# First stage of a hybrid decoder step: conditioning weights loaded in one piece, scale first, sums before squares

## Chip, cores, metric

One core of a Trainium2 chip runs the whole step as one program. The metric is device microseconds of one execution, from launch to end; lower is better. Engines: TensorE (PE, its weight loads PEld), VectorE (DVE), ScalarE (ACT), GpSimd (POOL) and SyncE (SP), which here only issues DMAs.

## What is computed

A two-layer decoder trunk (a gated linear attention layer, then a recurrent RG-LRU layer, each followed by a product-key expert mixer) for 256 prompt tokens and 8 x 4 sample tokens. Only the start matters here: a condition vector for each of nine sequences goes through Silu and the conditioning weights of a layer, which gives six vectors; the first two are the shift and the scale of the first norm, whose result enters the first projection.

```
cond = jax.nn.silu(c)
mod = (cond @ p['ada_w'][i] + p['ada_b'][i]).reshape(B, 6, D_MODEL)
sh1, sc1, g1, sh2, sc2, g2 = [mod[:, j, None, :] for j in range(6)]
hm = rms_norm(x, p['norm_mix_g'][i]) * (1 + sc1) + sh1
mixed, s_new = gla_mixer(hm, ...)          # begins with hm @ w_in
x = x + g1 * mixed
```

## The kernel before

Everything lies with the feature dimension on 128 partitions: x, hid and the like are [128, 8, 288] (8 pieces of the 1024 features, 256 prompt and 32 sample tokens). Products that matter are made in three matmuls of split operands: a high part (a rounded copy, made by ScalarE) and a low part (value minus high part, made by VectorE, in some stages by GpSimd), for weights (w_hi, w_lo, lines 660 and 1566) and for activations (hid_hi, hid_lo).

All weights stream in chunks of [128, 1024] floats (512 KB) through raw, a ring of four slots. SyncE issues them in the order of the list SEGMENTS, each as soon as the slot's last user is done (mix_freed, freed). The order of work on every engine is written out by hand, and semaphores join the engines; a wait holds up all that stands behind it on its engine.

The first stage: the segment ada_a holds 16 chunks, group 0 (shift) and group 1 (scale) of eight each. ada_chunk (line 1084) makes four small matmuls for each, with the condition as stationary operand, into a PSUM bank. ScalarE copies the sums to ada_row in two halves (ada_half, line 632), TensorE turns them (line 1091), VectorE adds the bias and writes mod (mods, line 1688). The other groups are mixed in between the 24 chunks of the first projection (MIX_ITEMS) and between those of later stages.

Ahead of it, ScalarE issues seven loads (lines 616 to 622) and waits for five of them together; it then makes Silu of the condition and eight squares of x. TensorE sums the squares (square_sum, line 1075), runs four filling matmuls into the PSUM banks (line 1298) and then the 16 chunks. VectorE makes the mean, the root with ScalarE's help, and once it has both groups, the coefficient (1 + scale) x gain (norm_coef). It then splits the first two main weights (next_low) and applies the norm (norm_apply): in the first norm, eight products x * coefficient * root (line 1606), then eight additions of the shift (line 1623), with ScalarE's high copies (line 715) and VectorE's low parts (line 1611) following piece by piece.

GpSimd waits for the use of all 16 chunks (raw_used), issues the eight loads of the sample states (line 557, 512 KB each), and makes the sample columns of the norm in three operations (norm_samples, lines 483 to 488); after ScalarE's copy of them (line 712) it makes their low part (line 490). TensorE's wait for that (smp_low) opens the loop over the 24 tiles of the first projection (three, lines 1062 to 1064), which also holds conditioning chunks and pieces of the attention (gla_piece; at tile 3 the low-rank projection, line 1372, reads hid itself).

The arena is one large buffer in which the stages lay out their tensors one over the other. Its first 16384 floats in each partition are not in use before the first projection writes its results there.

## Time and profile before

| | us |
|---|---|
| three runs, median | 2246.83 |
| three runs, lowest to highest | 2246.06 to 2248.22 |
| profiled execution, own time | 2247.59 |
| its span, first to last instruction | 2245.8 |

The profiled execution's own time is 1.8 us above its span, and 0.8 us above the median. Over the span TensorE is busy 2094.1 us, VectorE 1603.4, ScalarE 1334.3 and GpSimd 963.5. Times in the rows are microseconds from the start of the span. A timeline row gives the start, the length, the engine, the line of the kernel and the operation, and in square brackets how long the engine stood idle before it and which work ended that. Rows of one line close together are merged, and their count stands behind x. A plain 4-byte matmul leaves two records. The granted clock is a share of 2.4 GHz: 0.50 is 1.2 GHz.

### The profile page before, as it was taken

The numbers are of one execution on the slowest core, as the hardware profiler recorded it, in microseconds if no ns is written. First come the engines' busy times: TensorE is split into PE (matmuls) and PEld (weight loads), VectorE is DVE, ScalarE is ACT, GpSimd is POOL, SyncE is SP. The second block draws the span as 40 slices with busy tenths as digits, with TensorE's granted clock in tenths as the row PEclk, the third lists the DMA queues.
The fourth block names the chain that finished last, engine by engine and source line by source line (L and its number), as shares of the span: only waits on it lengthen the run. The fifth ranks groups of instructions, "written<-read, shape, count | busy, mean of one in ns | idle before, by whom it ended". The sixth has DMA issues, their size and how long they took to land.

```text
span 2245.8 us, 42297 instructions
## 1 busy us (share of the span) xinstructions
PE 2094.1 (93%) x14238; PEld 1844.4 (82%) x14238; DVE 1603.4 (71%) x2994; ACT 1334.3 (59%) x2370; POOL 963.5 (43%) x818
## 2 busy tenths in 40 slices
PE   4998899999999999999989579898999999999998
PEld 1777898989999987777769479898999998777776
DVE  1446565796888878777867453949799998877785
ACT  1444443456777767667744534455777776766774
POOL 1010027777888732223300000888777773222330
PEclk7999999999999999999999889999999999999999
DMA  7753536666555568888844344454533446888883
GB/s 268 267 190 126 177 114 225 235 225 222 190 182 196 198 228 297 296 305 293 294 154 141 107 134 131 133 177 153 198 127 130 131 131 203 302 299 302 294 293 126
DMA packets 125618, 459.89 MB, mean 205 GB/s; under 512 B 14144, under 2 KB 14672, under 8 KB 124480
## 3 DMA queue, kind: packets, MB, share of 16 engines
q1 hardware_dynamic: 103104, 377.14, 49.8%
q0 software_dynamic: 21504, 79.53, 9.6%
q10 hardware_dynamic: 896, 1.76, 0.2%
q8 instruction: 65, 1.06, 0.2%
q14 instruction: 49, 0.40, 0.1%
HBM read 449.93 MB, written 8.44 MB: 204 GB/s over the span
## 4 chain that ended last, share of the span: by engine, by line
PE 74%; DVE 8%; issue 6%; POOL 6%; ACT 3%; DMA 3%; POOLq 0%; ACTq 0%; DVEq 0%; SPq 0%
PE pm L1264 11%; PE pm L1266 11%; PE pm L1265 10%; PE pu L1194 7%; PE pu L1189 7%; PE pu L1190 6%; PE pu L1062 4%; POOL w_lo L506 3%; PE pu L1064 3%; PE pu L1063 3%; PE pm L1224 2%; PE pm L1225 2%; POOL w_lo L545 1%; PE pm L1084 1%; PE pu L1509 1%
## 5 line engine op out<-in xcount | busy, mean ns | idle before, releaser
L1566 DVE TENSOR_TENSOR w_lo<-raw,w_hi 128x1024 fp32r<-128x1024 f32 x492 | 627.3, 1275 | 418.2 <-ACT w_hi L660 367.9
L660 ACT ACTIVATE w_hi<-raw 128x1024 fp32r<-128x1024 f32 x604 | 637.5, 1056 | 445.0 <-PE pm L1266 225.2
L1189 PE MATMUL pu<-hid_hi,w_hi 128*128 128x256 f32 x2048 | 504.9, 287 | 8.4 <-ACT w_hi L660 8.4
L1190 PE MATMUL pu<-hid_lo,w_hi 128*128 128x256 f32 x2048 | 496.2, 281 | 0.0
L1189 PEld LDWEIGHTS pu<-hid_hi,w_hi 128*128 128x128 f32 x2048 | 388.8, 190 | 34.3 <-issue 31.0
L1264 PE MATMUL pm<-w_hi,hid_lo 128*128 128x512 f32 x1024 | 403.6, 394 | 2.2 <-DVE hid_lo L1807 2.2
L1266 PE MATMUL pm<-w_lo,hid_lo 128*128 128x512 f32 x1024 | 402.4, 393 | 0.0
L1265 PE MATMUL pm<-w_hi,hid_lo 128*128 128x512 f32 x1024 | 401.6, 392 | 0.0
L1190 PEld LDWEIGHTS pu<-hid_lo,w_hi 128*128 128x128 f32 x2048 | 388.6, 190 | 0.0
L506 POOL TENSOR_TENSOR w_lo<-raw,w_hi 128x1024 fp32r<-128x1024 f32 x112 | 299.8, 2687 | 201.0 <-ACT w_hi L660 200.2
L1194 PE MATMUL pu<-hid_hi,w_lo 128*128 128x256 f32 x2048 | 294.6, 286 | 16.3 <-POOL w_lo L506 15.7
L1194 PEld LDWEIGHTS pu<-hid_hi,w_lo 128*128 128x128 f32 x2048 | 260.9, 190 | 21.4 <-POOL w_lo L506 20.6
L545 POOL TENSOR_TENSOR w_lo<-oh_eq,sel_w 128x256 fp32r<-128x256 bf16 x256 | 219.3, 857 | 119.2 <-PE pm L1225 72.5
L1264 PEld LDWEIGHTS pm<-w_hi,hid_lo 128*128 128x128 f32 x1024 | 192.3, 188 | 70.0 <-issue 15.4
L1062 PE MATMUL pu<-hid_hi,w_hi 128*128 128x288 f32 x736 | 228.4, 310 | 22.7 <-POOL hid_lo L490 19.2
L1266 PEld LDWEIGHTS pm<-w_lo,hid_lo 128*128 128x128 f32 x1024 | 192.3, 188 | 43.7
L1063 PE MATMUL pu<-hid_lo,w_hi 128*128 128x288 f32 x736 | 221.0, 300 | 0.0
L1265 PEld LDWEIGHTS pm<-w_hi,hid_lo 128*128 128x128 f32 x1024 | 192.7, 188 | 33.4
L1064 PE MATMUL pu<-hid_hi,w_lo 128*128 128x288 f32 x736 | 220.1, 299 | 0.0
L794 ACT ACTIVATE w_lo<-const,sel_i 128x128 fp32r<-128x128 f32 x384 | 139.4, 394 | 125.8 <-PE pm L1225 125.4
L546 POOL TENSOR_TENSOR oh_lo<-oh_eq,sel_w 128x256 fp32r<-128x256 bf16 x256 | 211.7, 827 | 0.0
L526 POOL DMA_INDIRECT arena<-in_v_tab,sel_i x64 | 110.4, 1724 | 219.1 <-DVE arena L1833 174.1
(272 smaller groups left out, 3091.0 us busy)
## 6 DMA issues: line engine op xcount, KB each, us to landing
raw<-in_u_tab SPq DMA_DIRECT2D x256, 512.0 KB
raw<-in_v_tab SPq DMA_DIRECT2D x256, 512.0 KB
raw<-in_ada SPq DMA_DIRECT2D x96, 512.0 KB
raw<-in_wq SPq DMA_DIRECT2D x32, 512.0 KB
raw<-in_gla_in SPq DMA_DIRECT2D x24, 512.0 KB
raw<-in_rg_in SPq DMA_DIRECT2D x20, 512.0 KB
arena<-in_gla_state POOLq DMA_DIRECT2D x8, 512.0 KB, 10.4
raw<-in_gla_out SPq DMA_DIRECT2D x8, 512.0 KB
```

Source lines behind the costliest of these rows:

```text
L506: pool.tensor_tensor(w_lo[:, s % 2, :], raw[:, slot, :], w_hi[:, s % 2, :].bitcast(F32), ALU.subtract).then_inc(lo_pool, 1)
L660: act.activation(w_hi[:, s2, :], raw[:, s4, :], ACT.Copy).then_inc(hi_done, 1)
L1062: mm(out, w_hi[:, s2, cols], r_hi, start=(kk == 0), stop=False)
L1063: mm(out, w_hi[:, s2, cols], r_lo, start=False, stop=False)
L1064: return mm(out, w_lo[:, s2, cols], r_hi, start=False, stop=(stop and kk == n_k - 1))
L1189: mm(pu[:, s, 0:SEQ], w_hi[:, s % 2, kk * P:kk * P + P], hid_hi[:, kk, 0:SEQ], start=(kk == 0), stop=False)
L1190: mm(pu[:, s, 0:SEQ], w_hi[:, s % 2, kk * P:kk * P + P], hid_lo[:, kk, 0:SEQ], start=False, stop=False)
L1194: last = mm(pu[:, s, 0:SEQ], w_lo[:, s2, kk * P:kk * P + P], hid_hi[:, kk, 0:SEQ], start=False, stop=(kk == KD - 1))
L1264: mm(out, hid_lo[:, s, tok], w_hi[:, s % 2, cols], start=start, stop=False)
L1265: mm(out, hid_lo[:, 4 + s, tok], w_hi[:, s % 2, cols], start=False, stop=False)
L1266: last = mm(out, hid_lo[:, s, tok], w_lo[:, s % 2, cols], start=False, stop=stop)
L1566: tt_(w_lo[:, s2 if l2 is None else l2, :], raw[:, s4, :], w_hi[:, s2, :].bitcast(F32), ALU.subtract).then_inc(lo_done, 1)
```

## The change

The two conditioning groups of the first stage no longer go through the ring. Eight loads of two chunks each (1 MB) go into first_w, the free start of the arena, each with a semaphore of its own; the ring begins with the first projection's list. In memory the two first groups are swapped, so group 0 is now the scale and group 1 the shift. ScalarE's seven loads come in another order with counts of their own, and each user waits only for what it needs. TensorE runs its filling matmuls first, then the sums of group 0, the squares, and the sums of group 1. VectorE makes the coefficient and the eight products once the scale is there; the shift enters in the high copies (as a bias) and in the low parts, as in the later norms, and is added to hid itself only at step 2 of the projection. ScalarE splits the first main weight ahead of its copies and the second behind them.

```diff
--- before.py
+++ after.py
@@ -115,7 +115,7 @@
 _n = _m = _l = _u = _r = 0
 for _name, _c, _kind in SEGMENTS:
     STREAM[_name], SPLIT[_name], LOWS[_name], BANKED[_name], RAW[_name] = _n, _m, _l, _u, _r
-    _n += {"gla_in": len(MIX_ITEMS), "uv0": len(U0_ITEMS) + NKEY}.get(_name, _c)
+    _n += {"ada_a": 0, "gla_in": len(MIX_ITEMS), "uv0": len(U0_ITEMS) + NKEY}.get(_name, _c)
     _m += _c if _kind == "split" else 0
     _l += (_c - POOL_LOWS if _name[:2] == "uv" else _c) if _kind == "split" else 0
     _u += 0 if _name[:3] == "ada" else {"uv0": EARLY, "uv1": EARLY, "gates": 2 * RT, "gla_out": 0, "rg_out": 0}.get(_name, _c)
@@ -204,6 +204,7 @@
         ones = area(31264, P)
 
 
+        first_w = area(0, 2 * KD, D)
         proj = area(0, 24, T)
         q, k = proj[:, 0:4, :], proj[:, 4:8, :]
         vt, gt = proj[:, 8:16, :], proj[:, 16:24, :]
@@ -293,6 +294,11 @@
 
 
         raw_full = [sem(f"raw_full{s}") for s in range(RING)]
+        first_in = [sem(f"first_in{n}") for n in range(KD)]
+        cond_in = sem("cond_in")
+        const_in = sem("const_in")
+        x_in = sem("x_in")
+        hid_full = sem("hid_full")
         hi_done = sem("hi_done")
         lo_done = sem("lo_done")
         split_used = sem("split_used")
@@ -365,18 +371,16 @@
         OG_AT = [OG_ORDER.index(kk) for kk in range(KD)]
         NORM_OF = {0: "gla_in", 1: "wq0", 2: "rg_in", 3: "wq1"}
 
-        srcs = {"ada_a": ada[0:16], "gla_out": gla_out,
+        srcs = {"gla_out": gla_out,
                 "wq0": wq[0], "wq1": wq[1], "rg_in": rg_in[0:16], "rg_in2": rg_in[16:20], "gates": gates, "rg_out": rg_out}
         counts = {name: c for name, c, _ in SEGMENTS}
-        order = [name for name, _, _ in SEGMENTS]
+        order = [name for name, _, _ in SEGMENTS[1:]]
         GATE_OUTS = [3, 5]
 
         def freed(eng, name, c, first_half=False):
 
             if name == "gates":
                 eng.wait_ge(gate_used, 5 * (c // 2) + GATE_OUTS[c % 2])
-            elif name[:3] == "ada":
-                eng.wait_ge(raw_used, c + (RAW[name] + 1))
             elif first_half:
                 eng.wait_ge(lo_pool, c + (int(name[2]) * POOL_LOWS + 1))
             else:
@@ -400,6 +404,9 @@
 
         @block.sync
         def _(sp_):
+            for n in range(KD):
+                sp_.dma_start(first_w[:, 2 * n:2 * n + 2, :], ada[2 * n:2 * n + 2].rearrange("c p d -> p c d")).then_inc(
+                    first_in[n], 16)
             for n, name in enumerate(order):
                 total = counts[name]
 
@@ -485,6 +492,8 @@
                 pool.wait_ge(smp_own, 2 * n + 1)
                 pool.tensor_tensor(h_s, h_s, root_s, ALU.mult).then_inc(smp_own, 1)
                 pool.wait_ge(smp_own, 2 * n + 2)
+                if n == 0:
+                    pool.wait_ge(mod_ready, 2)
                 pool.tensor_tensor(h_s, h_s, shift_s, ALU.add).then_inc(smp_ready, 1)
                 pool.wait_ge(hh_ready, HIGH_BEFORE[NORM_OF[n]] + 3)
                 pool.tensor_tensor(hid_lo[:, :, SEQ:T], hid[:, :, SEQ:T], hid_hi[:, :, SEQ:T].bitcast(F32),
@@ -613,14 +622,14 @@
                 ins.then_inc(act_own, 1)
                 act.wait_ge(act_own, own[0])
 
-            act.dma_start(cond[:], ct).then_inc(consts_in, 16)
+            act.dma_start(cond[:], ct).then_inc(cond_in, 16)
+            act.dma_start(const[:], con[:, 0:2 * P]).then_inc(const_in, 16)
+            act.dma_start(x, xt).then_inc(x_in, 16)
             act.dma_start(parm[:], par).then_inc(consts_in, 16)
-            act.dma_start(x, xt).then_inc(consts_in, 16)
-            act.dma_start(const[:], con[:, 0:2 * P]).then_inc(consts_in, 16)
             act.dma_start(const_gla, con[:, 2 * P:CON_N]).then_inc(consts_in, 16)
             act.dma_start(lr_w, w_lr).then_inc(side_in, 16)
             act.dma_start(gate2, w_gate2).then_inc(side_in, 16)
-            act.wait_ge(consts_in, 80)
+            act.wait_ge(cond_in, 16)
             act.activation(cond[:], cond[:], ACT.Silu).then_inc(cond_ready, 1)
 
             def ada_half(g, half, acc):
@@ -639,12 +648,6 @@
                     last = act.activation(mod[:, g // 6, g % 6, kk, :], turned[:, at:at + NSEQ], ACT.Identity,
                                           bias=pcol("ada_b", g * KD + kk, g * KD + kk + 1))
                 last.then_inc(mod_ready, 1)
-
-            def ada_out(first, last):
-
-                for g in range(first, last):
-                    for half in range(2):
-                        ada_half(g, half, pu[:, ADA_BANK[g], :])
 
             def ada_step(c, acc, turned):
 
@@ -711,11 +714,8 @@
                         act.wait_ge(smp_ready, n + 1)
                         act.activation(hid_hi[:, :, SEQ:T], hid[:, :, SEQ:T], ACT.Copy).then_inc(hh_ready, 1)
                     act.wait_ge(hid_ready, n * KD + kk + 1)
-                    if n == 0:
-                        act.activation(hid_hi[:, kk, 0:SEQ], hid[:, kk, 0:SEQ], ACT.Copy).then_inc(hh_ready, 1)
-                    else:
-                        act.activation(hid_hi[:, kk, 0:SEQ], hid[:, kk, 0:SEQ], ACT.Identity,
-                                       bias=mod[:, lay, j_shift, kk, 0:1]).then_inc(hh_ready, 1)
+                    act.activation(hid_hi[:, kk, 0:SEQ], hid[:, kk, 0:SEQ], ACT.Identity,
+                                   bias=mod[:, lay, j_shift, kk, 0:1]).then_inc(hh_ready, 1)
 
             def out_ahead(name):
 
@@ -894,14 +894,20 @@
                     act.activation(v_tok_out[:, 2 * half, :], pm[:, 2 * half, :], ACT.Copy).then_inc(v_evac_act, 1)
 
 
+            act.wait_ge(x_in, 16)
             for kk in range(KD):
                 square(0, kk)
+            act.wait_ge(consts_in, 32)
             root_table()
+            ada_half(0, 0, pu[:, ADA_BANK[0], :])
             norm_root(0)
-            ada_out(0, 2)
-            for c in range(2):
-                next_high(0, c)
+            ada_half(0, 1, pu[:, ADA_BANK[0], :])
+            for half in range(2):
+                ada_half(1, half, pu[:, ADA_BANK[1], :])
+            next_high(0, 0)
+            act.wait_ge(mod_ready, 2)
             norm_high(0, 0, 0)
+            next_high(0, 1)
 
             def evac(n):
 
@@ -1090,16 +1096,18 @@
                 pe.wait_ge(ada_row_ready, 2 * g + half + 1)
                 pe.transpose(turned[:, half * P:half * P + P], ada_row[:], ident).then_inc(ada_tr, 1)
 
-            def ada_sums(name, g0):
-
-                full0, parts = (STREAM[name] // RING + 1) * 16, counts[name] // KD
-                for g in range(g0, g0 + parts):
-                    for kk in range(KD):
-                        ada_chunk(g * KD + kk, kk % 4, full0 + ((g - g0) * 2 + kk // 4) * 16, pu[:, ADA_BANK[g], :])
-                        if g > g0 and kk in (1, 3):
-                            turn(g - 1, kk // 2)
-                turn(g0 + parts - 1, 0)
-                turn(g0 + parts - 1, 1)
+            def first_sums(g):
+
+                for kk in range(KD):
+                    at, acc = g * KD + kk, pu[:, ADA_BANK[g], :]
+                    if at % 2 == 0:
+                        pe.wait_ge(first_in[at // 2], 16)
+                    for part in range(4):
+                        last = mm(acc[32 * part:32 * part + NSEQ, 0:256], cond[:, kk, :], first_w[:, at, part * 256:part * 256 + 256],
+                                  start=(kk == 0), stop=(kk == KD - 1), skip_group_check=True)
+                    last.then_inc(raw_used, 1)
+                    if g and kk in (1, 3):
+                        turn(g - 1, kk // 2)
 
             def turn(g, half):
 
@@ -1291,12 +1299,16 @@
 
 
             pe.wait_ge(ones_set, 1)
+            pe.wait_ge(const_in, 16)
+            for bank in range(4):
+                mm(pu[:, bank, 0:2 * P], ones, const[:], start=True, stop=True)
+            pe.wait_ge(cond_ready, 1)
+            first_sums(0)
             for kk in range(KD):
                 square_sum(0, kk)
-            pe.wait_ge(cond_ready, 1)
-            for bank in range(4):
-                mm(pu[:, bank, 0:2 * P], ones, const[:], start=True, stop=True)
-            ada_sums("ada_a", 0)
+            first_sums(1)
+            for half in range(2):
+                turn(1, half)
             pe.wait_ge(mod_ready, 2)
 
             def turns(n):
@@ -1368,6 +1380,7 @@
 
                 if j == 3:
                     pe.wait_ge(side_in, 32)
+                    pe.wait_ge(hid_full, KD)
                     for kk in range(KD):
                         last = mm(pm[0:RANK, 0, 0:T], lr_w[:, kk, :], hid[:, kk, :], start=(kk == 0), stop=(kk == KD - 1))
                     last.then_inc(lr_ready, 1)
@@ -1607,26 +1620,21 @@
 
                 def low_part(kk):
                     dve.wait_ge(hh_ready, HIGH_BEFORE[name] + kk + (1 if kk < 2 else 2))
-                    if n == 0:
-                        ins = tt_(hid_lo[:, kk, 0:SEQ], hid[:, kk, 0:SEQ], hid_hi[:, kk, 0:SEQ].bitcast(F32), ALU.subtract)
-                    else:
-                        ins = stt(hid_lo[:, kk, 0:SEQ], hid[:, kk, 0:SEQ], shift(kk), hid_hi[:, kk, 0:SEQ].bitcast(F32),
-                                  ALU.add, ALU.subtract)
-                    ins.then_inc(hl_ready, 1)
-
+                    stt(hid_lo[:, kk, 0:SEQ], hid[:, kk, 0:SEQ], shift(kk), hid_hi[:, kk, 0:SEQ].bitcast(F32),
+                        ALU.add, ALU.subtract).then_inc(hl_ready, 1)
+
+                for kk in range(KD):
+                    scaled(kk).then_inc(hid_ready, 1)
+                    if n and kk >= 2:
+                        low_part(kk - 2)
                 if n == 0:
-                    for kk in range(KD):
-                        last = scaled(kk)
-                    link(last)
-                for kk in range(KD):
-                    if n == 0:
-                        ts(hid[:, kk, 0:SEQ], hid[:, kk, 0:SEQ], shift(kk), None, ALU.add).then_inc(hid_ready, 1)
-                    else:
-                        scaled(kk).then_inc(hid_ready, 1)
-                    if kk >= 2:
-                        low_part(kk - 2)
-                for kk in (KD - 2, KD - 1):
+                    mods(1, 2)
+                    dve.wait_ge(mod_ready, 2)
+                    next_low(0, 0)
+                for kk in range(KD - 2 if n else 0, KD):
                     low_part(kk)
+                if n == 0:
+                    next_low(0, 1)
 
             def inverse_root(r, m, t):
 
@@ -1685,8 +1693,9 @@
                     dve.wait_ge(ada_tr, 2 * g + 2)
                     by_half = "p (part half) b -> p part half b"
                     turned = pu[:, ADA_BANK[g], 2 * P:4 * P].rearrange("p (half part b) -> p part half b", half=2, part=4)
-                    tt_(mod[:, g // 6, g % 6].rearrange(by_half, half=2), turned[:, :, :, 0:NSEQ],
-                        bc(pcol("ada_b", g * KD, g * KD + KD), P, KD, NSEQ).rearrange(by_half, half=2),
+                    j = 1 - g if g < 2 else g
+                    tt_(mod[:, j // 6, j % 6].rearrange(by_half, half=2), turned[:, :, :, 0:NSEQ],
+                        bc(pcol("ada_b", j * KD, j * KD + KD), P, KD, NSEQ).rearrange(by_half, half=2),
                         ALU.add).then_inc(mod_ready, 1)
 
             def route(lay, tt):
@@ -1880,13 +1889,13 @@
                         ALU.add).then_inc(x_ready, 1)
 
 
-            dve.wait_ge(consts_in, 80)
+            dve.wait_ge(consts_in, 32)
+            dve.wait_ge(const_in, 16)
+            dve.wait_ge(x_in, 16)
             norm_inverse(0)
-            mods(0, 2)
-            dve.wait_ge(mod_ready, 2)
+            mods(0, 1)
+            dve.wait_ge(mod_ready, 1)
             norm_coef(0, pcol("mix_g", 0, KD), 0, 0)
-            for c in range(2):
-                next_low(0, c)
             norm_apply(0, 0, 0)
 
             def state_chunk(c):
@@ -1912,6 +1921,9 @@
 
             def gla_step(j):
 
+                if j == 2:
+                    for kk in range(KD):
+                        ts(hid[:, kk, 0:SEQ], hid[:, kk, 0:SEQ], mod[:, 0, 0, kk, 0:1], None, ALU.add).then_inc(hid_full, 1)
                 if j == 3:
                     dve.memset(sc_s, 0.0)
                 if j == 7:
@@ -2146,7 +2158,7 @@
         "par": np.concatenate([cols(parts[n]) for n in PAR_COLS], axis=1),
         "con": con,
 
-        "ada": w["ada_w"].reshape(2, KD, P, 6, D).transpose(0, 3, 1, 2, 4).reshape(96, P, D),
+        "ada": w["ada_w"].reshape(2, KD, P, 6, D).transpose(0, 3, 1, 2, 4).reshape(12, KD, P, D)[[1, 0, *range(2, 12)]].reshape(96, P, D),
         "gla_in": chunks(main_in),
         "w_lr": w["gla_w_in"][0][:, 3 * D:].reshape(KD, P, RANK).transpose(1, 0, 2),
         "w_gate2": w["gla_w_gate2"][0],
```

## Rows read from the trace of the kernel before

**Rows 1.** Page, part 1: busy time, share of the span, instructions; TensorE first.
```profile
PE 2094.1 (93%) x14238; PEld 1844.4 (82%) x14238; DVE 1603.4 (71%) x2994; ACT 1334.3 (59%) x2370; POOL 963.5 (43%) x818
```

**Rows 2.** TensorE in windows: length, busy (instructions), granted clock, DMA share, GB/s.
```profile
60.00:70.00 10.00, 10.00 (x80) 0.86 0.76 249
```

**Rows 3.** Timeline of the start: start us, length us, instruction [idle before it].
```profile
0.76 2.17 SPq L415 DMA_DIRECT2D raw<-in_ada  x4
...
12.56 0.26 ACT L624 ACTIVATE cond<-cond 128x72 f32<-128x72 f32 x1 [6.65 <-DMA arena<-in_con]
...
13.30 6.67 PE L1075 MATMUL pm<-arena 128*128 128x288 f32 x16 [13.30 <-ACT arena L705]
...
19.80 1.89 PE L1298 MATMUL pu<-const,arena 128*128 128x256 f32 x8
...
21.62 1.92 PE L1084 MATMUL pu<-raw,cond 128*9 128x256 f32 x32
```

**Rows 4.** Line 1075 in windows 15:17 and 19:22: ns min/median/max, first and last start.
```profile
L1075 PE MATMUL pm<-arena x6: 687/687/687, 14.4 to 16.8; 128*128 128x288 f32 x6
...
L1075 PE MATMUL pm<-arena x4: 406/406/406, 18.8 to 19.6; 128*128 128x288 f32 x4
```

**Rows 5.** Timeline, the last conditioning sum on TensorE.
```profile
43.73 1.04 PE L1084 MATMUL pu<-raw,cond 128*9 128x256 f32 x8 [0.53 <-DMA raw<-in_ada]
```

**Rows 6.** Windows, all engines: busy (instructions) of each, granted clock, DMA share, GB/s.
```profile
10.00:12.50 2.50, 0.00 (x0) 0.00 (x0) 0.00 (x0) 0.00 (x0) 0.00 (x0) 1.00 0.85 315
...
20.00:22.50 2.50, 2.50 (x25) 1.60 (x27) 1.76 (x4) 0.44 (x1) 0.00 (x0) 1.00 0.00 0
...
22.50:25.00 2.50, 1.04 (x20) 0.33 (x12) 0.07 (x1) 0.00 (x0) 0.00 (x0) 1.00 0.59 195
...
27.50:30.00 2.50, 1.00 (x12) 0.25 (x16) 0.00 (x0) 0.00 (x0) 0.00 (x0) 0.74 0.94 360
...
55.00:57.50 2.50, 0.00 (x0) 0.00 (x0) 2.46 (x7) 0.00 (x0) 0.00 (x0) 0.50 1.03 418
```

**Rows 7.** DMA queues in 7.5:10 (packets, MB, share); issues, KB, us to landing.
```profile
q10 hardware_dynamic: 93, 0.67, 63.9%
q1 hardware_dynamic: 98, 0.34, 33.3%
...
arena<-in_xt ACTq DMA_DIRECT2D x1, 1152.0 KB, 9.5
...
parm<-in_par ACTq DMA_DIRECT2D x1, 111.0 KB, 5.4
```

**Rows 8.** Timeline, from the last conditioning sum to the first main tile.
```profile
45.12 4.41 POOL L557 DMA_DIRECT2D arena<-in_gla_state  x8 [44.16 <-PE pu L1084]
...
46.53 0.23 DVE L1688 TENSOR_TENSOR mod<-pu,parm 128x72 f32<-128x72 f32 x1 [7.27 <-PE pu L1091]
...
51.23 0.64 POOL L488 TENSOR_TENSOR arena<-arena,mod 128x256 f32<-128x256 f32 x1
...
54.08 3.25 DVE L1606 SCALAR_TENSOR_TENSOR arena<-arena,coef 128x256 f32<-128x256 f32 x8
...
58.38 0.40 ACT L712 ACTIVATE hid_hi<-arena 128x256 fp32r<-128x256 f32 x1
...
58.86 0.95 POOL L490 TENSOR_TENSOR hid_lo<-arena,hid_hi 128x256 fp32r<-128x256 f32 x1 [6.99 <-ACT hid_hi L712]
...
61.73 0.61 PE L1062 MATMUL pu<-hid_hi,w_hi 128*128 128x288 f32 x1
```

**Rows 9.** Timeline, shift passes and the second main weight against its tile.
```profile
57.37 0.88 DVE L1623 TENSOR_SCALAR arena<-arena,mod 128x256 f32<-128x256 f32 x3
...
59.14 0.81 DVE L1623 TENSOR_SCALAR arena<-arena,mod 128x256 f32<-128x256 f32 x1
...
67.11 1.23 DVE L1566 TENSOR_TENSOR w_lo<-raw,w_hi 128x1024 fp32r<-128x1024 f32 x1 [4.36 <-ACT w_hi L660]
...
70.10 0.40 PE L1062 MATMUL pu<-hid_hi,w_hi 128*128 128x288 f32 x1
```

## The prediction, made before the change was run

> **What bounds the kernel now.** I read the page first: TensorE is busy 93% of the span [rows 1], so what counts is where it stands still, and the change touches only its first 62 us. From the first main tile on it does not: the ten windows of 10 us from 60 to 160 us all read 10.00 busy, the first of them stands for all [rows 2]. What is late before that tile shifts the rest one for one, and what is saved there is saved at the end unless the ring of weights stumbles.
>
> Second view, the start in order of time [rows 3]. SyncE issues its four ring loads at 0.76 us, then must wait for a used slot. ScalarE waits for all five of its own loads and begins at 12.56; TensorE sums squares for 6.67 us from 13.30, runs four filling matmuls, and touches the first conditioning weights at 21.62. Third view, the DMA in windows [rows 6]: 0 GB/s in the window at 20 us (and none from about 12.5 on), 195 in the one after it. So the ring stands still for 10 us, and afterwards the last conditioning chunk starts at 43.73 for 1.04 us: the sums end at t = 44.77 [rows 5]. Fourth view, what follows [rows 8]: GpSimd starts only then, issues eight state loads (4.41 us) and makes the sample columns until 51.87; VectorE splits two weight chunks and scales x from 54.08; ScalarE copies the sample columns at 58.38, GpSimd takes their low part until 59.81, TensorE runs two chunks and reaches tile 0 at 61.73. Tile 0 stands 16.96 us behind t.
>
> **The change, part by part.**
>
> *Loads ahead of use.* The 16 ring loads become eight of 1 MB into the arena, which wait for nothing, and four ring loads (first main weights, two later conditioning chunks, second main weights) right behind. 8.39 MB must land before the sums can end. The two queues share: in 7.5 to 10 us ScalarE's moved 0.67 MB and SyncE's 0.34 [rows 7]. SyncE's four loads, 2.10 MB, and ScalarE's 1.8 MB ended together near 12.5 us. The window 10 to 12.5 is not full (315 GB/s), so about 0.2 MB more fits: 2.3 MB by 12.5. Windows with a DMA share near one give 360 (0.94) and 418 GB/s (1.03) [rows 6]; I take 410, since nothing will pace these loads. The first group (4.19 MB) is then there at 12.5 + 1.9/0.41 = 17.1 us, the whole 8.39 MB at 12.5 + 6.1/0.41 = 27.4, and the second main weights 5.1 us later, far ahead of their use. At 360 the last is there at 29.4.
>
> *Constants in another order.* x keeps nearly its place (issued at 1.7 us or a little later, 9.5 to land [rows 7], so about 11.3). The small constants move ahead of it; parm, second in line before, took 5.4 us [rows 7], so I put them at 7. The condition goes by its own count, so its Silu is off the path. TensorE's four filling matmuls, 1.89 us at full clock and up to twice that cold [rows 3], run from 7 to about 10.5, while TensorE would wait for weights anyway: nothing on the path.
>
> *Sums first, squares after.* The first group's sums follow the loads and end one pair of chunks behind the last: a chunk costs 1.92/4 = 0.48 us at full clock [rows 3], 1.04 cold [rows 5], 1.08 with a gap; 18.2 to 19.3 us. Squares were ready at about 14. The square sums cost 6.67 us as one piece that began cold and ended warm [rows 3]. Their records start 0.48 us apart in the cold part and 0.27 in the warm one [rows 4]; 16 records make 7.7 us all cold, 4.2 all warm. I take 6.7, the same mix: the clock can fall ahead of them, as it fell from 2.4 to 1.2 GHz in the window 27.5 to 30, when TensorE got its chunks one by one from the DMA [rows 6], and rise again under them. They end at 25.4. Then the second group's eight chunks, three quarters of them landed: 8 x 0.55 (with gaps) plus two turned halves, 5.0 us. The sums end at t = 30.4, 1 us or more behind the last landing.
>
> *Scale ahead of shift.* The root of the mean, the scale (group 0), the coefficient and eight products (3.25 us [rows 8]) now run on VectorE beside the second group's sums: mean at 25.5, root and its two corrections to 28.1, products from 29 to 32.3. The shift arrives as long behind the last sum as before, 46.76 - 44.77 = 2.0 us [rows 8], so at 32.4. The products and the separate shift pass leave the stretch behind t. The shift is folded into the high and the low copies, which cost what they cost. ScalarE splits main weight 0 ahead of the copies and 1 behind them.
>
> *Next behind t.* GpSimd's order is unchanged: it waits for all 16 chunks, issues eight state loads, and only then scales the samples: t + 7.10 (51.87 - 44.77 [rows 8]). It becomes the last one: ScalarE's copy 0.40, its own low part 0.95, two gaps of 0.08, and 1.92 from there to tile 0 (two chunks at cold clock) [rows 8]; tile 0 starts at t + 10.5, against 16.96 before. The main copies end inside it (0.4 us each behind the sample copy, as fast as a tile eats them), and the second weight is split 2 us before tile 1. Tile 0: 30.4 + 10.5 = 40.9 us against 61.73 [rows 8]: 20.8 us saved, 14.4 of them from the earlier t and 6.4 from work moved ahead of it.
>
> *Added behind tile 0.* For the low-rank projection VectorE adds the shift to hid in eight passes at step 2 (0.88/3 = 0.29 us each [rows 9], 2.3 us), between the low parts of main weights 2 and 3. Before, weight 2 was split at 68.34 and its tile began at 70.10 [rows 9]; weight 3 follows a tile later, so the 2.3 us fit in VectorE's idle time. Without that cover tile 3 would wait 0.5 to 2 us. The load of main weight 3 now waits for the late split of weight 1, some 1.2 us later than before against tile 0, with two tiles to spare.
>
> A rule that speaks against the size of this: the Trainium skill, DMA: Bandwidth & Descriptors, "Where 436 GB/s comes from", lets loads from HBM be bound at about 358 GB/s for a core. The window at 418 [rows 6] exceeds it, so the measurement decides; by 358 the last group would land 2.2 us later, of which 1 is free, and the sum would be 19.6 us.
>
> **Sum.** 2247.59 (the profiled execution) - 20.8 = 2226.8; the median of the three runs is 0.8 below that execution, so I forecast 2246.83 - 20.8 = 2226.0 us.
>
> **The rivals.**
>
> *Clock kept, loads bind.* If the clock stays full through the trickle, the squares take 4.2 us and t follows the last landing: 27.4 + 1.1 = 28.5, tile 0 at 39.0, or 38 if GpSimd's gap leaves the clock up too. 2223 to 2224 us. Against it: the fall in the window 27.5 to 30 [rows 6]. Chance 0.13.
>
> *Clock low throughout.* Sums to 19.3, squares 7.7, eight chunks at 1.08 and two turns: t = 36.6, tile 0 at 47. Gain 14.7, 2232 us. For it: after its fall the clock still stood at half at 57 us [rows 6], through all later sums. Against: under the dense square sums of before the pace went from the cold to the warm one [rows 4]. Chance 0.16.
>
> *State loads in the way.* They start at 31 us and need about 12 us (4.2 MB at 0.41 and 2 us to land), so they still run at tile 0, where before they had ended. Main weight 2 is asked for just before tile 0 and shares the DMA with them, as in 7.5 to 10 us [rows 7]: 0.5 MB at half rate is 2.6 us and some 2 more to land, about the 4.3 us after which ScalarE wants it (its high copy ended at 67.11, 5.4 us behind tile 0's start, after about 1 us); the split weight then has 1.8 us to spare [rows 9]. Late by 1 to 3 us: 2227 to 2230. In the same case: GpSimd slower in its issues, which now run beside VectorE's products and split, at most by their length, 3 us. The Trainium skill, SBUF — State Buffer, "Who interferes with whom", has certain VectorE operations and GpSimd shut each other out of a shared port for a whole instruction; the trace agrees where one shift pass beside GpSimd's low part took 0.81 us, not 0.29 [rows 9], and shows no such loss in the issues themselves. Chance 0.17.
>
> *The large loads run slowly.* One mechanism on the other side: 1 MB loads of two chunks in one instruction, a shape that the start has not shown, get less than the ring's small ones. At 195 GB/s, the worst window [rows 6], t = 12.5 + 31.3 + 1.1 = 44.9, tile 0 at 55.4, and 6 us are still won (2240). Slower than before begins where t passes 61.7 - 10.5 = 51.2, below 6.1/37.6 = 162 GB/s; at 150 the time is 2250. Rows of 4 KB on each side speak against it. Chance 0.04, half of that slower.
>
> *It does not do what it says* (something keeps the first loads or the second group behind x, so that the idle 10 us stay): only the 6.4 us behind t, 2240. Nothing queues ahead of SyncE's loads; chance 0.02.
>
> **Numbers.** Forecast 0.48; rivals as above. The range takes in the forecast with its bounds (t by 1 to 2 us from rate and clock phase), the kept clock and the low clock: 2222.5 to 2232.5; outside lie the slow loads and the tails. A measurement here tells about 0.2% (4.5 us): faster by more 0.95, within 0.02, slower 0.03.
>
> **What would show it.** In the profile after: no 0 GB/s window before 30 us; TensorE's squares starting at 18 to 20; end of the second group's sums at 30 to 31; VectorE's products over by then; GpSimd's state loads issued from there and its sample columns 7.1 us behind; tile 0 at 41; steady tiles after it with no wait for a DMA. The prediction is wrong if tile 0 lies outside 38 to 48 us, if tiles 1 to 4 wait for weights, or if the shift at tile 0 is not the shift of the end.

## The result and the profile after

| | before | after |
|---|---|---|
| runs beside each other, median us | 2247.02 (4 runs) | 2221.88 (4 runs) |
| lowest to highest | 2246.06 to 2248.22 | 2219.85 to 2224.29 |
| profiled execution, own time | 2247.59 | 2222.51 |
| its span | 2245.8 | 2220.7 |

The ratio of the times is 0.9888, with a 95% interval of 0.9871 to 0.9905. The change saves 25.1 us; forecast were 20.8. The time lies 0.6 us below the low end of the range. Unchanged copies of both kernels, run later, gave 2222.34 (0.9886, 0.9869 to 0.9902) for after and 2245.14, one execution, for before.

The page of after, part 1, answers to [rows 1]. TensorE's busy time is the same as before to 0.2 us (2093.9 against 2094.1), so the whole gain is time in which it stood still.

```profile
PE 2093.9 (94%) x14238; PEld 1848.8 (83%) x14238; DVE 1596.8 (72%) x2994; ACT 1335.7 (60%) x2370; POOL 985.1 (44%) x818
```

The timeline of after from the start to tile 0 (start us, length us, engine, line and operation, idle time before it and what ended that) answers to [rows 3], [rows 5] and [rows 8].

```profile
7.21 3.75 PE L1304 MATMUL pu<-const,arena 128*128 128x256 f32 x8 [7.21 <-DMA const<-in_con]
...
18.12 1.05 PE L1106 MATMUL pu<-arena,cond 128*9 128x256 f32 x16 [1.92 <-DMA arena<-in_ada]
...
19.10 4.15 PE L1081 MATMUL pm<-arena 128*128 128x288 f32 x16
...
26.45 3.26 DVE L1619 SCALAR_TENSOR_TENSOR arena<-arena,coef 128x256 f32<-128x256 f32 x8
...
27.12 1.05 PE L1106 MATMUL pu<-arena,cond 128*9 128x256 f32 x16 [1.39 <-DMA arena<-in_ada]
...
29.67 1.89 PE L1106 MATMUL pu<-arena,cond 128*9 128x256 f32 x16 [1.50 <-DMA arena<-in_ada]
...
31.91 4.40 POOL L566 DMA_DIRECT2D arena<-in_gla_state  x8 [30.95 <-PE pu L1106]
...
38.01 0.64 POOL L497 TENSOR_TENSOR arena<-arena,mod 128x256 f32<-128x256 f32 x1
38.68 0.42 ACT L715 ACTIVATE hid_hi<-arena 128x256 fp32r<-128x256 f32 x1 [4.19 <-POOL arena L497]
...
39.18 0.73 POOL L499 TENSOR_TENSOR hid_lo<-arena,hid_hi 128x256 fp32r<-128x256 f32 x1 [0.53 <-ACT hid_hi L715]
...
40.00 1.90 PE L1090 MATMUL pu<-raw,cond 128*9 128x256 f32 x16 [6.72 <-issue]
41.83 0.61 PE L1068 MATMUL pu<-hid_hi,w_hi 128*128 128x288 f32 x1
```

The reader is to see three things. The conditioning sums now end at t = 29.67 + 1.89 = 31.56 us, where they ended at 44.77 [rows 5]. The last two pairs of chunks each wait for their load (the releaser is DMA arena<-in_ada), so the loads bind; the last pair then runs at half clock (1.89 us, the pair before it 1.05), which adds 0.8 us. Behind t GpSimd is the last one, with the same steps as before: TensorE starts again 0.1 us after its low part ends at 39.91. This trace names no releaser there; the second execution of after has, in the same place, 7.02 us of waiting that POOL hid_lo L499 ends. Tile 0 starts at 41.83, 10.27 us behind t, where it was 16.96.

The windows of after answer to [rows 6] (length, busy time and instructions of PE, PEld, DVE, ACT and POOL, granted clock, DMA share, GB/s). The window at 20 us, 0 GB/s before, moves 413, and between 12.5 and 30 us TensorE's clock falls only in the window at 27.5. The 1.00 ahead of 12.5 us does not fit the work there: the four filling matmuls took 3.75 us, and 1.89 before, where they ran at full clock [rows 3].

```profile
10.00:12.50 2.50, 2.50 (x27) 0.91 (x29) 0.00 (x0) 1.17 (x4) 0.00 (x0) 1.00 1.03 406
...
20.00:22.50 2.50, 2.50 (x12) 1.98 (x11) 0.00 (x0) 0.00 (x0) 0.00 (x0) 1.00 1.03 413
22.50:25.00 2.50, 2.50 (x33) 1.06 (x35) 0.99 (x3) 0.72 (x2) 0.00 (x0) 1.00 1.01 397
...
27.50:30.00 2.50, 1.00 (x20) 0.24 (x12) 2.20 (x6) 0.00 (x0) 0.00 (x0) 0.80 1.04 415
```

To follow the gain through the program I set the same TensorE instruction, counted from the end of the program, of both traces side by side. Each cell is how much earlier than in the first trace of before it starts (us); the heads are that instruction's start in before.

| kernel | 61.7 (tile 0) | 70 (tile 2) | 100 | 201 | 600 | 1130 | 1190 | 1650 | 1860 | 2200 |
|---|---|---|---|---|---|---|---|---|---|---|
| after | 19.9 | 18.5 | 17.0 | 17.1 | 17.8 | 18.1 | 19.9 | 20.4 | 25.2 | 25.1 |
| after, again | 20.0 | 19.3 | 19.0 | 19.2 | 19.5 | 17.8 | 18.9 | 20.7 | 25.5 | 24.9 |
| before, again | 1.8 | 1.2 | 1.2 | 1.1 | 1.5 | 1.3 | 3.4 | 2.7 | 2.7 | 2.5 |

So 19.9 us are saved at tile 0 against this one execution of before (18.1 against the second), 1.4 are lost over the first two tiles (0.7 in the second execution of after), and all but 4.8 of the rest is drift of a size that an unchanged kernel shows between two executions. The 4.8 us come in one place, between 1650 and 1860 us, in both traces of after and in neither of before. That stretch is the late part of layer 1's expert mixer, whose code the change doesn't touch.

### The profile page after: what moved, and what is told of

Its sections match the earlier page's. It is cut to its first block, busy times and chain, and to the rows that moved or that the text cites. A ratio compares the mean times of both kernels' runs of the same rounds, so it can differ in the third digit from the quotient of the medians.

```text
span 2220.7 us, 42254 instructions
## 1 busy us (share of the span) xinstructions
PE 2093.9 (94%) x14238; PEld 1848.8 (83%) x14238; DVE 1596.8 (72%) x2994; ACT 1335.7 (60%) x2370; POOL 985.1 (44%) x818
## 4 chain that ended last, share of the span: by engine, by line
PE 79%; DVE 7%; issue 5%; POOL 4%; ACT 2%; DMA 2%; SPq 0%; POOLq 0%; DVEq 0%; ACTq 0%
PE pm L1272 11%; PE pm L1274 11%; PE pm L1273 11%; PE pu L1202 8%; PE pu L1197 8%; PE pu L1198 8%; PE pu L1068 4%; PE pu L1069 3%; PE pu L1070 3%; POOL w_lo L515 3%; PE pm L1232 3%; PE pm L1233 2%; PE pm L1090 1%; PE pu L1522 1%; DMA arena<-in_ada 1%
## 5 line engine op out<-in xcount | busy, mean ns | idle before, releaser
L1579 DVE TENSOR_TENSOR w_lo<-raw,w_hi 128x1024 fp32r<-128x1024 f32 x492 | 637.6, 1296 | 431.5 <-ACT w_hi L663 372.6
L555 POOL TENSOR_TENSOR oh_lo<-oh_eq,sel_w 128x256 fp32r<-128x256 bf16 x256 | 256.3, 1001 | 0.0
L1068 PE MATMUL pu<-hid_hi,w_hi 128*128 128x288 f32 x736 | 229.7, 312 | 22.7 <-POOL hid_lo L499 19.2
L554 POOL TENSOR_TENSOR w_lo<-oh_eq,sel_w 128x256 fp32r<-128x256 bf16 x256 | 195.6, 764 | 92.6 <-PE pm L1233 43.5
```

The costliest lines, as they stand in the source:

```text
L1068: mm(out, w_hi[:, s2, cols], r_hi, start=(kk == 0), stop=False)
L1579: tt_(w_lo[:, s2 if l2 is None else l2, :], raw[:, s4, :], w_hi[:, s2, :].bitcast(F32), ALU.subtract).then_inc(lo_done, 1)
```

## Experiments

Three questions: what made t, what is last behind it, and what saved 4.8 us in a loop 1600 us away. "Against after" is the difference of two medians, each taken beside runs of before whose medians lay between 2246.6 and 2248.2.

**Repeats.** The two copies without an edit set the scale for all single traces: 1 to 3 us of a trace's offsets are of that execution alone.

> The kernel before, unchanged, profiled once more. The 8.1 us that the changed kernel gained behind the first stage lie in three places: the expert loops of layer 0 (1.0), the squares at the start of layer 1 (1.9) and the late expert loop of layer 1 (5.2). Theory chance (these places fall one way or the other from execution to execution, whatever the kernel): this profile may show the late loop of layer 1 as fast as the changed kernel's. Theory bound to the kernel: tile for tile as in the first profile, within 0.5 us at every place, first main tile at 61.7, execution 2246 to 2248 us.

> The changed kernel, unchanged, five rounds and a second profile. Its four runs spread over 4.4 us, those of the kernel before over 2.2. Theory chance: this profile shows the late loop of layer 1 about 5 us slower than the first profile did, or the clock dip near 70 us missing (1.3 us faster), and single runs spread over 4 to 7 us. Theory bound to the kernel: the same places, total 2220 to 2224, ratio 0.988 to 0.990.

Measured: the late loop is bound to the kernel. It takes 209.9 us in both executions of before and 205.1 in both of after. The first stage and the squares at the start of layer 1 are not: before_again reaches tile 0 at 59.90, 1.8 us earlier than the first execution and outside the 0.5 that the second theory allows, and gains 2.1 us between 1130 and 1190. after_again gave 2222.34 and has no clock dip near 70 us.

**Paced loads.** Is it the time of the loads that makes the gain, or the order of the work?

```diff
             for n in range(KD):
+                if n >= 2:
+                    sp_.wait_ge(raw_used, 2 * n - 2)
                 sp_.dma_start(first_w[:, 2 * n:2 * n + 2, :], ...
```

> The changed kernel, but each large load from the third on waits until the pair of chunks two before it has been used, so that two are in flight as in a ring; order and arithmetic of all engines are the changed kernel's. Theory A (loads ahead of use are what moved the end of the conditioning sums): idle DMA windows come back, the sums end at 35 to 38 instead of 31.6, tile 0 at 45 to 48, total 4 to 6 us higher, 2226 to 2228. Theory B (the order of constants, sums and squares did it): the end stays within 1 us, total unchanged. On the late loop of layer 1, theory bound to the kernel's instructions: it stays in its fast form (4.8 us under the kernel before); theory bound to when the first stage ends: it may fall back.

Measured: 2231.21 us (0.993, 0.9913 to 0.9947), 9.3 us worse than after, and tile 0 at 51.00. Its windows (columns as above) show the half empty stretches that after doesn't have, at 69, 174 and 172 GB/s:

```profile
12.00:16.00 4.00, 2.87 (x33) 0.95 (x32) 0.00 (x0) 3.50 (x9) 0.00 (x0) 1.00 0.27 69
16.00:20.00 4.00, 1.11 (x12) 0.44 (x16) 0.00 (x0) 0.75 (x2) 0.00 (x0) 0.68 1.01 416
26.00:30.00 4.00, 4.00 (x24) 2.60 (x26) 0.29 (x1) 0.00 (x0) 0.00 (x0) 0.79 0.43 174
30.00:34.00 4.00, 2.04 (x30) 0.66 (x22) 3.25 (x10) 0.72 (x2) 0.00 (x0) 1.00 0.58 172
```

So with everything else in after's order, waiting for use costs 9.2 us at t (40.7 against 31.6) and at tile 0; both theories had less (A up to 6). The loads ahead of use carry 9.2 of the 13.2 us by which t moved. The other 4.0 are there with paced loads too, and no run divides them between the order of the small loads, the order of the sums and the size of the loads. Part of the 9.2 is clock: TensorE ran these sums and squares partly at half clock (6.31 us for the squares).

**Squares first.** Does the new order on TensorE matter?

```diff
-            first_sums(0)
             for kk in range(KD):
                 square_sum(0, kk)
+            first_sums(0)
             first_sums(1)
```

> TensorE sums the squares ahead of the first group's chunks instead of behind them; nothing else is changed. Theory A (the last landing of the eight large loads, near 29.6, sets the end of the sums): the sums end at 31 to 32 us all the same, tile 0 at 41 to 42, total the same within 1 us. Theory B, that of the prediction (TensorE's own work of fill, sums and squares sets it): the order does not change its sum, so the end stays as well, but the windows show TensorE waiting for loads in the second group for 1 us in A against none in B. If instead the squares hold up the scale, the products on VectorE end later than the shift and tile 0 moves; then total 1 to 3 us higher.

Measured: 2221.69 us (0.9885, 0.9868 to 0.9902), no difference. TensorE's timeline shows why: the squares start at 12.88 and take 6.14 us instead of 4.15, but the last two pairs wait for their loads all the same.

```profile
12.88 6.14 PE L1081 MATMUL pm<-arena 128*128 128x288 f32 x16 [0.96 <-ACT arena L708]
...
28.10 1.90 PE L1106 MATMUL pu<-arena,cond 128*9 128x256 f32 x16 [2.72 <-DMA arena<-in_ada]
30.66 1.90 PE L1106 MATMUL pu<-arena,cond 128*9 128x256 f32 x16 [0.66 <-DMA arena<-in_ada]
```

The order of squares and sums is worth nothing here: both lie ahead of the last load.

**Products late, weights first.** Two undo parts of VectorE's new order. The first puts the wait for the shift ahead of the eight products; the second also puts the split of both main weights ahead of them, as in before.

```diff
+                if n == 0:
+                    mods(1, 2)
+                    dve.wait_ge(mod_ready, 2)
                 for kk in range(KD):
                     scaled(kk).then_inc(hid_ready, 1)
                 ...
                 if n == 0:
-                    mods(1, 2)
-                    dve.wait_ge(mod_ready, 2)
                     next_low(0, 0)
```

```diff
+                if n == 0:
+                    mods(1, 2)
+                    dve.wait_ge(mod_ready, 2)
+                    next_low(0, 0)
+                    next_low(0, 1)
                 for kk in range(KD):
                     scaled(kk).then_inc(hid_ready, 1)
```

> The changed kernel, but VectorE makes the eight products of the norm only after the shift has come, not beside the second group's sums: 3.3 us of VectorE work go back behind the sums. Theory A (GpSimd's state loads and sample columns are the last thing before tile 0): they hide it; tile 0 at 41.5 to 42.2, total unchanged within 1 us. Theory B (VectorE's chain is last or nearly so): tile 0 2 to 3 us later and the total 2224 to 2226.

> The changed kernel with the old order behind the sums: ScalarE and VectorE split both first main weights before anything else, and the eight products come after them; the loads stay early. Theory A (GpSimd's 7.1 us behind the sums hide VectorE's chain, so the new order has no share in the gain): VectorE's low parts begin near 40 and keep ahead of tile 0 at half clock; tile 0 at 41.5 to 42.5, total 2221 to 2223. Theory B (the order brought part of the 6.6 us): tile 0 2 to 4 us later, total 2224 to 2226.

Measured: products_late 2222.34 (0.989, 0.9873 to 0.9906), no difference in the time. Its tile 0, at 42.48, lies 11.2 us behind its t of 31.3, 0.9 more than in after and just outside what theory A allowed. weights_first 2227.29 (0.9912, 0.9895 to 0.9929), 5.4 us worse. But its tile 0 is at 42.66, only 0.8 us later than after's, and at 201 us it is 18.1 us ahead of before, inside what the two traces of after show (17.1 and 19.2). What it lacks is the step at 1650 to 1860: 19.3 and 19.2 us ahead there. That is the late loop (below), not the order. Neither expectation had this.

Near tile 0 it shows what the order is worth. t is about 30.7 here, so tile 0 stands 12.0 us behind it, 1.7 more than in after. GpSimd's second sample operation takes 1.53 us beside VectorE's split, against 0.72 in after, where VectorE is idle:

```profile
35.81 1.51 DVE L1579 TENSOR_TENSOR w_lo<-raw,w_hi 128x1024 fp32r<-128x1024 f32 x1 [1.78 <-ACT w_hi L663]
36.36 1.53 POOL L493 TENSOR_TENSOR arena<-arena 128x256 f32<-128x256 f32 x1
37.24 4.57 DVE L1619 SCALAR_TENSOR_TENSOR arena<-arena,coef 128x256 f32<-128x256 f32 x8
```

**What is next behind t.** GpSimd's eight state loads (4.40 us) stand ahead of the sample columns. samples_first swaps them. samples_spaced also holds back state load b until main weight b + 3 is used up. kept_busy leaves GpSimd alone and gives TensorE ten filling matmuls behind the last turn. samples_spaced_busy is samples_spaced with five of these, and samples_wide_busy has wider steps, b + b // 2.

```diff
+            norm_samples(0, 0, 0)
             for b in range(8):
+                pool.wait_ge(split_used, b + 3)      # samples_spaced; samples_wide_busy: 3 + b * 3 // 2
                 pool.dma_start(...)
-            norm_samples(0, 0, 0)
```

```diff
             for half in range(2):
                 turn(1, half)
+            for _ in range(10):                      # kept_busy; 5 in the two *_busy ones
+                mm(pm[:, 1, 0:2 * P], ones, const[:], start=True, stop=True)
```

> GpSimd makes the sample columns of the first norm before it issues the eight state loads. Theory A (what ends last behind the conditioning sums is GpSimd, held by 4.4 us of issues): the shift of the sample columns ends at about t + 2.7 instead of t + 7.1, first main tile at t + 6, about 37.5 instead of 41.8, with t = 31.6; total 4 us lower, 2217 to 2218, more if the shorter gap lets the clock rise earlier. Theory B (VectorE's and ScalarE's chain of weight 0, high copies and low parts is nearly as late): first main tile no earlier than 39.5, total 2 us lower or less. Theory C (state loads now collide with main weights 2 and 3 on the DMA): tile 0 earlier but tiles 2 to 4 wait, and the total is unchanged.

> GpSimd makes the sample columns first, as in samples_first, and issues the eight state loads one by one, each after one more tile of the projection from tile 2 on; they are used 15 tiles in. Theory A (samples_first won 3.4 us at tile 0 and gave them back because the state loads pushed the weights of tiles 2 to 5 aside): tile 0 at 38 to 38.5, no wait of TensorE before tile 6, and the 3 us are still there at 100 us and at the end, total 2218 to 2219.5. Theory B (what took them back was the clock, or the ring itself cannot deliver weights so early): tiles 2 to 5 wait all the same and the total stays at 2221 to 2224.

> The changed kernel with ten filling matmuls (256 columns, a free PSUM bank) behind the last turned half, where TensorE stands idle for 6.7 us before the sample columns are ready. Theory A (the clock, down at 1.2 GHz over the idle stretch, costs 2.5 to 3 us in the two conditioning chunks and tile 0): with the fill ending before 40 us the clock is at 2.4 GHz at tile 0, the chunks take 1.1 instead of 1.9 us and tile 0 takes 3.4 instead of 5.1; the gain at tile 1 is 2 to 2.5 us and the total 2219.5 to 2220. Theory B (the clock is up only after the tiles themselves have run for a while): tile 0 unchanged, total unchanged. If the fill runs over 40 us it delays tile 0 by what it overhangs.

> Sample columns first, state loads spaced one to a tile, and five filling matmuls in the remaining 3 us gap. Theory A (both gaps, order and clock, add up): tile 0 at 37.5 to 38.5, tile 0 in 3.4 to 4 us, total 2216 to 2218.5, the lowest so far. Theory B (the dips of the clock in the low-rank pieces later on take away what is won here, wherever they fall): gain at tile 1 is there, total no lower than 2219.

> Sample columns first, five filling matmuls, state loads one to every one and a half tiles from tile 2 to 12. Theory A (the 3 us lost near 83 to 90 us in the last such kernel came from state loads beside the ring): no wait for conditioning chunks before 100 us, 24 us ahead of the kernel before at 100 us and at the end 28 to 29 with the fast late loop, total 2218 to 2220. Theory B (the ring's need of about 300 GB/s leaves no room for 4 MB at all): the same 3 us are lost elsewhere, total 2221.

| kernel | median us | ratio, 95% | us ahead of before at tile 0 | at 201 |
|---|---|---|---|---|
| after | 2221.88 | 0.9871 to 0.9905 | 19.9 | 17.1 |
| samples_first | 2224.12 | 0.9874 to 0.9911 | 23.3 | 17.2 |
| samples_spaced | 2222.91 | 0.9879 to 0.9912 | 24.1 | 21.1 |
| kept_busy | 2224.91 | 0.9879 to 0.9912 | 21.6 | 18.0 |
| samples_spaced_busy | 2221.04 | 0.9865 to 0.9898 | 23.9 | 20.5 |
| samples_wide_busy | 2220.14 | 0.9867 to 0.9900 | 24.2 | 20.7 |

Each comes to tile 0 earlier than after, by up to 4.3 us. At the end none is told apart from after: samples_first and kept_busy are 2 to 3 us behind it, samples_wide_busy is 1.7 us ahead, and all the intervals overlap. Against the expectations: samples_first did what its theory C says. samples_spaced and samples_spaced_busy reached tile 0 as early as theory A had it, and missed its totals (2218 to 2219.5 and 2216 to 2218.5). kept_busy was to win 2 us or nothing and came out 3.0 us behind. samples_wide_busy, at 2220.14, does not tell its two theories apart.

The timeline of samples_first shows where its 3.4 us go. The state loads are issued one after the other until 40.9 us, and the ring's loads share the DMA with them:

```profile
36.48 4.44 POOL L567 DMA_DIRECT2D arena<-in_gla_state  x8
...
38.47 0.61 PE L1068 MATMUL pu<-hid_hi,w_hi 128*128 128x288 f32 x1
...
44.94 1.06 ACT L663 ACTIVATE w_hi<-raw 128x1024 fp32r<-128x1024 f32 x1 [1.86 <-DMA raw<-in_gla_in]
...
49.05 0.62 PE L1090 MATMUL pu<-raw,cond 128*9 128x256 f32 x8 [2.48 <-DMA raw<-in_ada]
```

ScalarE waits for a main weight, then TensorE waits 2.48 us for a conditioning chunk, and in the windows right behind this hole its clock is down again. By 100 us 6 of the 23 us are gone:

```profile
48.00:50.00 2.00, 0.95 (x11) 0.52 (x12) 1.36 (x6) 0.00 (x0) 0.00 (x0) 1.00 1.02 416
50.00:52.00 2.00, 2.00 (x11) 2.00 (x11) 0.00 (x0) 0.40 (x1) 0.00 (x0) 0.58 1.02 414
52.00:54.00 2.00, 2.00 (x11) 2.00 (x10) 1.31 (x2) 0.65 (x1) 0.00 (x0) 0.57 1.03 412
```

kept_busy meets the same queue from the other side: its clock is full at the first main tile, so it asks for weights earlier, and ScalarE waits 3.87 us for one and TensorE 2.31 for a chunk. In after TensorE has no such wait and ScalarE waits at most 0.8 us for a main weight. kept_busy issues its state loads in after's place and meets the waits all the same, so that place alone does not keep after free of them. What after has besides is a tile 0 that comes 1.7 us later and runs its first 4 us at half clock, which gives the DMA time; no run separates these two. Spacing the state loads removes the first hole and spreads the rest: samples_spaced is still 23.7 us ahead at 100 us and 21.1 at 201. Its profiled execution was its fastest by far (2219.58, median 2222.91), so the trace flatters it. What the spaced versions are worth stays open within about 3 us.

**The late loop.** The step at 1650 to 1860 us was first seen in the traces. An untouched loop, far behind the change: I suspected the place of its instructions, since the change alters the number of instructions ahead of it. So I gave before waits that are already fulfilled where they stand, and do no work.

```diff
 # before_more_waits: all of these; before_pool_wait: the first alone
+                if n == 0:
+                    pool.wait_ge(mod_ready, 2)
 # before_vector_wait: this alone (before_more_waits has it too)
+            dve.wait_ge(cond_ready, 1)
 # before_two_vector_waits: that one and
+            dve.wait_ge(ones_set, 1)
 # before_more_waits has besides
+            act.wait_ge(ones_set, 1)
+            pe.wait_ge(consts_in, 80)
+            pe.wait_ge(sq_ready, 1)
```

after_vector_wait is after with the one `dve.wait_ge(cond_ready, 1)`, just ahead of `norm_inverse(0)`.

> The kernel before, with waits that are already fulfilled added in the first stage: one each on GpSimd, VectorE and ScalarE, two on TensorE, so that each engine has as many instructions ahead of layer 1 as in the changed kernel. Nothing waits longer for it. Theory A (where the late expert loop of layer 1 lies in the instruction stream sets in which of two rhythms VectorE and GpSimd fall): the loop becomes 4 to 5 us faster, total 2241 to 2243. Theory B (the rhythm comes from something else that the change carries, or from the state in which the loop is entered): the loop as in the kernel before, total 2246 to 2248.

> The kernel before with one fulfilled wait more, on GpSimd alone. Theory A (the rhythm of the late loop of layer 1 depends on where GpSimd's loop lies in its instruction stream): loop in the fast form, 205.1 us from its start to its end instead of 210. Theory B (another engine's place decides): 210.

> The kernel before with one fulfilled wait more, on VectorE alone. Theory A (GpSimd's place decides): the loop as before, 210 us. Theory B (VectorE's place decides): 205.1.

> The kernel before with two fulfilled waits more on VectorE. Theory A (the place decides): with two it may be either form, and the same one as the changed kernel with one more wait, since VectorE's stream is then equally long in both. Theory B (any shift): fast form, 205.1 us.

> The changed kernel with one fulfilled wait more on VectorE. Theory A (the place of the late loop of layer 1 in VectorE's stream decides its rhythm, and the changed kernel only happens to stand one instruction further than the kernel before): the loop may leave its fast form, 210 us instead of 205.1, and the total rises by 4 to 5 us to 2226 to 2227; first stage unchanged. Theory B (any shift away from the place in the kernel before gives the fast form): 205.1 us and 2221 to 2223.

| kernel | us | VectorE instructions | 1650 to 1860, us |
|---|---|---|---|
| before (and again) | 2247.0 | 3922 | 209.9, 209.9 |
| before_pool_wait | 2246.43, one execution | 3922 | 210.0 |
| before_vector_wait | 2243.70, one execution | 3923 | 205.1 |
| before_two_vector_waits | 2239.86, one execution | 3923 | 205.1 |
| before_more_waits | 2243.06 (10 runs), 0.9978, 0.9969 to 0.9988 | 3923 | 205.1 |
| after (and again) | 2221.9 | 3923 | 205.1, 205.1 |
| after_vector_wait | 2226.76, 0.9912, 0.9895 to 0.9929 | 3924 | 209.9 |
| weights_first | 2227.29, 0.9912, 0.9895 to 0.9929 | 3924 | 210.0 |

The instructions are all that the trace has for VectorE, waits included. The two waits of before_two_vector_waits left one instruction more, not two, so its count is 3923; I had meant it as the case of two. The other eight changed kernels of this study, all made from after, have 3923 and take 205.1 or 205.2.

One fulfilled wait on VectorE makes before 4.8 us faster in this loop and after 4.8 us slower; one on GpSimd does nothing. The time agrees: ten runs of before_more_waits, which has waits on the other engines as well, are 0.22% faster than before (interval clear of 1), and the four of after_vector_wait stand 4.9 us above the median of after, with no overlap between the two sets of runs. In all 18 traces the loop goes with the count of VectorE's instructions, odd or even. What in VectorE or in the fetching of its instructions makes a place count is not shown by any row, and that it is parity is a reading of three counts.

How the loop differs once it runs is in the rows. GpSimd's operations in the window 1660 to 1800 us, grouped by line (busy us, mean ns, idle us before them), first before, then before_vector_wait, then after, then after_vector_wait:

```profile
L545 POOL TENSOR_TENSOR w_lo<-oh_eq,sel_w 128x256 fp32r<-128x256 bf16 x70 | 64.2, 916 | 36.0 <-PE pm L1225 18.0 <-DVE oh_eq L1764 18.0
L546 POOL TENSOR_TENSOR oh_lo<-oh_eq,sel_w 128x256 fp32r<-128x256 bf16 x69 | 48.2, 699 | 0.0
```

```profile
L546 POOL TENSOR_TENSOR oh_lo<-oh_eq,sel_w 128x256 fp32r<-128x256 bf16 x70 | 77.0, 1100 | 0.0
L545 POOL TENSOR_TENSOR w_lo<-oh_eq,sel_w 128x256 fp32r<-128x256 bf16 x71 | 48.6, 685 | 19.2 <-DVE oh_eq L1764 19.2
```

```profile
L555 POOL TENSOR_TENSOR oh_lo<-oh_eq,sel_w 128x256 fp32r<-128x256 bf16 x70 | 77.1, 1102 | 0.0
L554 POOL TENSOR_TENSOR w_lo<-oh_eq,sel_w 128x256 fp32r<-128x256 bf16 x71 | 48.6, 684 | 18.6 <-DVE oh_eq L1773 18.6
```

```profile
L554 POOL TENSOR_TENSOR w_lo<-oh_eq,sel_w 128x256 fp32r<-128x256 bf16 x68 | 61.8, 909 | 34.0 <-DVE oh_eq L1773 18.0 <-PE pm L1233 16.0
L555 POOL TENSOR_TENSOR oh_lo<-oh_eq,sel_w 128x256 fp32r<-128x256 bf16 x69 | 48.2, 698 | 0.0
```

In the slower rhythm the slow operation is the first product of a pair, and GpSimd waits for TensorE as well; in the faster one it is the second product, and the wait for TensorE is gone. The timelines say the same. GpSimd in before, then in after:

```profile
1701.44 1.64 POOL L545 TENSOR_TENSOR w_lo<-oh_eq,sel_w 128x256 fp32r<-128x256 bf16 x1
...
1708.35 0.76 POOL L545 TENSOR_TENSOR w_lo<-oh_eq,sel_w 128x256 fp32r<-128x256 bf16 x1 [2.00 <-PE pm L1225]
1709.07 0.61 POOL L546 TENSOR_TENSOR oh_lo<-oh_eq,sel_w 128x256 fp32r<-128x256 bf16 x1
```

```profile
1700.42 1.59 POOL L555 TENSOR_TENSOR oh_lo<-oh_eq,sel_w 128x256 fp32r<-128x256 bf16 x1
1702.54 0.76 POOL L554 TENSOR_TENSOR w_lo<-oh_eq,sel_w 128x256 fp32r<-128x256 bf16 x1 [0.53 <-DVE oh_eq L1773]
...
1704.40 1.59 POOL L555 TENSOR_TENSOR oh_lo<-oh_eq,sel_w 128x256 fp32r<-128x256 bf16 x1
```

In longer stretches of the same views, after repeats itself every 3.99 us (1702.54, 1706.53) with one stretched product of 1.59 us in four. before repeats every two such steps, 8.20 us (1700.15, 1708.35). The stretched products lie beside VectorE's split of a weight (1.23 us where nothing runs beside it, 1.65 in after's rhythm). The Trainium skill, SBUF — State Buffer, "Who interferes with whom", has VectorE operations with two inputs in SBUF and GpSimd operations that read SBUF shut each other out of one port; these rows agree (1.59 us for an operation of 0.61), and so does the 1.53 against 0.72 in weights_first.

## Why the prediction was right and wrong

| step | forecast | measured |
|---|---|---|
| fill on TensorE | 7 to 10.5 | 7.21 to 10.96 |
| group 0 sums end | 18.2 to 19.3 | 19.17 |
| squares | 6.7 us, to 25.4 | 4.15 us, to 23.25 (4.15 to 6.3 us in other traces) |
| products | 29 to 32.3 | 26.45 to 29.71 |
| last large load seen | 27.4 | 29.67 |
| t | 30.4 | 31.56 |
| shift ready | t + 2.0 | t + 2.0 (33.55) |
| sample columns | t + 7.1 | t + 7.1 (38.65) |
| tile 0 | t + 10.5 = 40.9 | t + 10.3 = 41.83 |
| shift pass | 2.3 us, hidden | 2.19 us, hidden |
| saved at tile 0, saved at the end | 20.8, 20.8 | 19.9, 25.1 |

*Right.* The mechanism in the main: loads that wait for nothing (paced_loads undoes that and loses 9.3 us), and GpSimd as the last one behind t, where the samples come at t + 7.1 to 0.1 us. The shift pass at step 2 started at 50.07, between the splits of weights 2 and 3, and no TensorE wait follows from it between 42 and 70 us. The small constants were ready at 7, and x at 11.3.

*Two terms mis-sized, in opposite ways.* The squares: the forecast took the mixed pace of before, since it expected the clock to fall ahead of them as in [rows 6]. It was 1.00 in all windows from 12.5 to 27.5, and they took 4.15 us, the all warm figure. The waits of 1.85 and 1.92 us between pairs of chunks did not bring the clock down in this execution. In another trace it fell: with the same order and waits of 1.5 and 1.8 us, after_vector_wait has half clock from 19.8 to 23.3 us and 5.84 us for the squares. With one trace of each kernel it stays open whether the kernel or the execution decides that. The landing: by bytes alone the last of 8.39 MB was due at 27.4, and the rate was as assumed (391 to 419 GB/s in nearly all windows from 7.5 us on, one of 372). But a load is not there when its bytes could be. Up to 29.6 us the queue of SyncE had moved 9.20 MB, with the last of the 8.39 MB just in:

```profile
q1 hardware_dynamic: 2388, 9.20, 79.1%
q10 hardware_dynamic: 896, 1.76, 15.8%
```

0.8 MB of the loads queued behind had already come. At 410 GB/s that is 2.0 us, nearly all of the 2.3 us by which I was early. The first error would have made t 28.5 ("Clock kept, loads bind"); the later landing and a last pair at half clock (0.8 us) put it to 31.56. So the case that came true is that rival with a later landing, and that the forecast t was right to 1.2 us is luck, made of two wrong terms. The length of the squares had no weight: squares_first spends 6.14 us on them ahead of the sums for the same total, and after_vector_wait 5.84 us in after's place and ends its sums at 30.7.

Nor did the eight loads leave at once. SyncE issued seven by 4.3 us and the eighth only at 8.3; the DMA moved 406 to 430 GB/s from 5 to 12.5 us all the same.

*The order behind t.* The prediction gave 6.4 us to work moved ahead of GpSimd's chain, and 6.7 came (5.5 against before_again, where tile 0 lies 15.7 us behind t). The number is right, the reason only in part. In before, what held up VectorE behind t was the second main weight. ScalarE waited for its load until 51.85, and the split, the products from 54.08 and the shift passes queued behind it:

```profile
51.85 1.06 ACT L660 ACTIVATE w_hi<-raw 128x1024 fp32r<-128x1024 f32 x1 [4.94 <-DMA raw<-in_gla_in]
```

The prediction has no such wait. weights_first puts splits and products back behind the shift but keeps the loads early, and its tile 0 lies 11.9 us behind t, so the order gives only 1.7 of the 6.7 us (0.9 by products_late). Of the other 5.0, 2.8 are the second main weight, there in time: the products start 6.5 us behind t (37.24) instead of 9.3 (54.08). The last 2.2 fall, by subtraction, to the shift folded into the copies; no run takes that alone.

*Named but not seen.* "State loads in the way": in after the profile names no wait of TensorE between 42 and 70 us. The rival is real, though: it bites as soon as tile 0 comes 1.7 to 3.4 us earlier, in kept_busy and samples_first. "The large loads run slowly" did not happen: 1 MB loads run at the rate of the ring's.

*The step that failed*: "what is saved there is saved at the end unless the ring of weights stumbles". The ring did not stumble, 19.9 us were saved at tile 0 and 25.1 at the end. What put the result out of the range is the late loop of layer 1, 1600 us behind the change, which gave 4.8 us. The sum has no term for it. The loop's time goes with the number of VectorE's instructions, which the change alters by one. after_vector_wait has the whole change but the loop's old rhythm, and there the step holds: 20.8 us ahead at tile 0 (at 40.95, forecast 40.9), 21.3 at the end. Its median is 2226.76, 0.8 us from the forecast of 2226.0. The first stage is worth what was forecast, within what can be measured (the interval is 16 to 24 us), and the loop 4.8 on top.

The same step also failed in the small, and more by the execution than by the kernel. In the first trace of after 1.4 us were lost in tiles 0 and 1, which ran their first 4.3 us at half clock; in before the clock rose 1.1 us behind tile 0's start. In the second executions the two times are 2.9 and 2.4 us. The prediction said that the clock might be low in the sums, and did not carry it into the first tile. A further 1.5 us went between 70 and 74 us in the first trace of after, where the clock fell under a TensorE that was busy throughout:

```profile
68.00:70.00 2.00, 2.00 (x15) 1.01 (x14) 1.23 (x1) 1.22 (x3) 0.00 (x0) 0.99 0.04 16
70.00:72.00 2.00, 2.00 (x9) 2.00 (x10) 0.00 (x0) 1.08 (x3) 0.00 (x0) 0.50 0.44 102
72.00:74.00 2.00, 2.00 (x12) 2.00 (x11) 0.00 (x0) 0.00 (x0) 0.00 (x0) 0.65 0.97 381
```

The second execution of after has 1.00 in the same windows, and before_more_waits has such a dip at 90 to 94 us. It belongs to an execution, not to the kernel.

*Still open*: why the loop's rhythm goes with VectorE's instruction count; what made the 4.0 us of t that paced_loads keeps; and some 2 us between 1130 and 1650 us, which both kernels show in one execution and not in another.

## What to carry to other kernels

Where a start-up stage loads through a ring and the queue stands at 0 GB/s in the middle of it, use free space for loads that need no used slot, see what the next loads in the queue gain by it (here 2.8 us through the second main weight), and don't expect the last of them by bytes alone (here 2 us later). When a producer is made earlier, look at the transfers that then meet: here up to 4.3 us gained at tile 0 never showed at the end, and in two of these cases the trace has the weights waiting behind the state loads. And carry a small gain through the whole trace by the same instruction in both kernels: a fifth of this one was not where the change was, and an idle wait instruction could give it or take it.

## What the hardware did that was not expected

- One fulfilled wait on VectorE near the start changes the time of a loop 1600 us later by 4.8 us, in either direction (209.9 and 205.1 us for the same work). A wait on GpSimd does not.
- A load at the end of a queue landed when the queue had moved 9.20 MB, though 8.39 MB stood up to and with it.
- With no other core in the program, one core loaded at 391 to 419 GB/s in most windows from 7.5 to 32.5 us (372 in the slowest). The Trainium skill, DMA: Bandwidth & Descriptors, "Where 436 GB/s comes from", has loads from HBM bound at about 358 for a core; the windows here are above it for 20 us on end, and the measurement decides.
- TensorE's clock fell to 0.50 and 0.65 in two windows while it was busy in all of them, in one execution and not in the next, at a price of 1.5 us.
- With the same work in the same order on TensorE, the granted clock was 1.00 in the window at 20 us in after and 0.50 in after_vector_wait (squares 4.15 and 5.84 us). No run shows why.
